# First modulation made as columns, x normalised and turned tile by tile, parameters and narrow weights laid out as runs, first weights in four loads, running sums behind the evictions

## What is computed

```python
cond = jax.nn.silu(c)                                  # c: 1 x 1024
mod = cond @ ada_w[layer] + ada_b[layer]               # 1024 x 6144
sh1, sc1, g1, sh2, sc2, g2 = [m[:, None, :] for m in jnp.split(mod, 6, axis=-1)]
h = rms_norm(x, norm_mix[layer]) * (1 + sc1) + sh1     # x: 512 x 1024
qa, ka, va, ga, za, qkvb, ab, bb, zb = _split(h @ w_in, AB_SPLITS)
```

## Time and profile before

| | before |
|---|---|
| time, median of 3 runs | 1469.92 us (1468.84 to 1470.89) |
| the profiled execution's own time | 1473.01 us |
| its span in the trace | 1470.8 us |
| PE busy | 1282.0 us (87%) |
| DVE busy | 1099.5 us (75%) |
| ACT busy | 700.2 us (48%) |
| first product of the projections | at 42.5 us |
| end of block n = 0 | at 77.8 us |
| end of `project_ab` on PE | at 244.7 us |

### The profile page before, as it was taken

One profiled execution on the slowest core, in us unless ns is written; L12 is line 12 of the kernel. 1 busy time (PEld: TensorE's weight loads), 2 busy tenths in 40 slices (PEclk: granted clock), 3 DMA queues, 4 the chain that ended last, 5 costly groups with the idle time before them and its releaser, 6 DMA issues. The chain is left out here.

```text
span 1470.8 us, 15601 instructions
## 1 busy us (share of the span) xinstructions
PE 1282.0 (87%) x6032; PEld 974.7 (66%) x6032; DVE 1099.5 (75%) x1340; ACT 700.2 (48%) x899; POOL 301.6 (21%) x125
## 2 busy tenths in 40 slices
PE   5886997869999959999999968986898799999992
PEld 3565885659884557888888854444446588888882
DVE  2756886667783666999999946967357499999994
ACT  3221334122251316777777814127422377777770
POOL 2000000000000001466455410000000145645431
PEclk9998998879999959999999978997996799999996
DMA  9688536011603267999999646354006499999944
GB/s 336 221 292 276 190 100 198 32 44 58 258 1 129 75 231 264 374 387 383 373 378 367 232 162 234 121 208 171 0 29 257 151 366 378 377 389 383 382 189 187
DMA packets 63728, 337.65 MB, mean 230 GB/s; under 512 B 11837, under 2 KB 12350, under 8 KB 49572
## 3 DMA queue, kind: packets, MB, share of 16 engines
q1 hardware_dynamic: 51428, 311.00, 57.1%
q0 software_dynamic: 11360, 22.39, 4.3%
q10 hardware_dynamic: 864, 3.23, 0.6%
HBM read 325.11 MB, written 28.84 MB: 241 GB/s over the span
## 5 line engine op out<-in xcount | busy, mean ns | idle before, releaser
L2491 DVE TENSOR_TENSOR ring_r<-ring,early_mod_r 128x2048 fp32r<-128x2048 f32 x76 | 197.8, 2633 | 25.7 <-ACT early_mod_r L1594 25.2
L1441 PE MATMUL ps<-ring_r,work_r 128*128 128x512 f32 x536 | 212.2, 396 | 0.0
L1594 ACT ACTIVATE work<-ps 128x512 f32<-128x512 f32 (+3 forms) x125 | 84.7, 683 | 236.0 <-PE ps L1441 133.0
L1439 PE MATMUL ps<-early_mod_r,work_r 128*128 128x512 f32 x468 | 187.7, 401 | 10.3 <-DVE work_r L2794 4.7
L1440 PE MATMUL ps<-early_mod_r,work_r 128*128 128x512 f32 x468 | 183.7, 393 | 0.0
L1594 ACT ACTIVATE work_r<-ring 128x2048 fp32r<-128x2048 f32 (+2 forms) x87 | 133.8, 1558 | 95.6 <-PE ps L955 95.0
L852 POOL TENSOR_TENSOR work<-work,early_mod 128x1024 f32<-128x1024 f32 x30 | 142.7, 4756 | 146.6 <-ACT work L1594 146.6
L1594 ACT ACTIVATE early_mod_r<-ring 128x2048 fp32r<-128x2048 f32 x79 | 147.5, 1908 | 0.3 <-PE ps L1441 0.2
L1439 PE MATMUL ps<-work_r 128*128 128x512 f32 x324 | 132.2, 408 | 6.8 <-DVE work_r L2794 4.7
L946 PE MATMUL ps<-const,work 128*128 128x128 f32 (+1 forms) x680 | 100.1, 289 | 41.1 <-DMA work<-h_rows,row_i 11.7
L1440 PE MATMUL ps<-work_r 128*128 128x512 f32 x324 | 128.8, 397 | 0.0
(11 more groups left out here) (334 smaller groups left out, 2452.3 us busy)
## 6 DMA issues: line engine op xcount, KB each, us to landing
ring<-in_moe_w_up_dram SPq DMA_DIRECT2D x33, 2048.0 KB, 10.0
early_mod<-in_ada_w_dram SPq DMA_DIRECT2D x80, 512.0 KB, 4.5
ring<-in_moe_w_gate_dram SPq DMA_DIRECT2D x19, 2048.0 KB, 9.7
hT<-in_moe_w_down_dram SPq DMA_DIRECT2D x16, 2048.0 KB, 9.7
ring<-in_moe_w_down_dram SPq DMA_DIRECT2D x15, 2048.0 KB, 9.9
work<-in_moe_w_gate_dram SPq DMA_DIRECT2D x14, 2048.0 KB, 10.1
ring<-in_ab_w_in_dram SPq DMA_DIRECT2D x7, 2048.0 KB, 9.5
ring<-in_ada_w_dram SPq DMA_DIRECT2D x3, 2048.0 KB, 20.4
```

Source lines behind the costliest of these rows:

```text
L1439: mm(out, a_lo, w_hi, start=first_, stop=False)
L1441: return mm(out, a_hi, w_lo, start=False, stop=last_)
L1594: return nc.scalar.activation(out, in_, fn, **kw)
L2491: v.tensor_tensor(half_of(l, m, half, True), half_of(l, m, half), highs[(2 * m + half) % MHIGHS].bitcast(F32), ALU.subtract).then_inc(SV.s ...
```

## The change

The pieces of the modulation are made as columns directly: PE takes 128 columns of a row block of `ada_w` as weights and `cond` as a single moving column, 16 products for the four row blocks and 4 for `part[i]`, each with one output column; the bias comes as columns with `cond` and is added by DVE. The repeated `cond`, the diagonal and the reduction go. Each tile of x gets its own root, is scaled by DVE into `h` and turned by PE as a plain transpose; ACT puts tile t - 1 away after it has squared tile t. On PE all four turns now stand ahead of the modulation's products. The first weights of `project_ab` come in four loads of 512 KB with a semaphore each. The parameters are laid out on the host as one block, and it and the early constants are loaded by SP behind the four pieces of `ada_w`; the narrow weights are laid out so that each partition's are one run. In `project_ab` the sums of a quarter follow its copies, and `per_step` is changed.

```diff
-        per_step = {0: (0, 0, 3, 3), 1: (0, 0, 0, 0), 2: (3, 3, 3, 3), 3: (2, 3, 2, 3), 4: (1, 1, 1, 2), 5: (1, 1, 1, 2), 6: (1, 1, 1, 2), 7: (2, 2, 1, 0)}
+        per_step = {0: (0, 0, 2, 2), 1: (0, 0, 0, 1), 2: (3, 3, 3, 2), 3: (3, 3, 3, 2), 4: (1, 1, 1, 2), 5: (1, 1, 1, 2), 6: (1, 1, 1, 2), 7: (2, 2, 2, 0)}
...
+        def narrow(of, c):
+            return of[:, c % RING].rearrange("p k f -> p (k f)")[:, 0:KD * SMALL].rearrange("p (k f) -> p k f", k=KD)
...
-                    free(c)
-                    sp.dma_start(slot(c)[:, :, 0:RANK], rows(a["ab_w_in"][0], slice(C_GA, C_GA + RANK))
-                                 ).then_inc(small_in, 16)
-                    load(c, slot(c)[:, :, RANK:RANK + 8], rows(a["ab_w_in"][0], slice(C_AB, C_AB + 8)))
+                    load(c, narrow(ring, c).rearrange("p k f -> p (k f)"), a["small_cols"])
...
-            load_ab(0)
+            for q in range(4):
+                sp.dma_start(ring[:, 0, 2 * q:2 * q + 2], rows(a["ab_w_in"][0], slice(0, 512))[:, 2 * q:2 * q + 2]).then_inc(ab0_in[q], 16)
             load_first(2)
             load_first(3)
+            sp.dma_start(block_in, a["params"]).then_inc(early_in, 16)
+            sp.dma_start(early_mod[:, 0:NEARLY], a["consts"][:, 0:NEARLY]).then_inc(early_in, 16)
...
-            param(w2aug[0:SMALL + 1, :], a["gate_rows"])
-            param(conv_w.rearrange("p c k -> p (c k)"), a["conv_cols"])
-            param(gla_gain, bc(a["gla_norm"][0]))
...
-            param(dt_bias, bc(a["gdn_dt_bias"][0]))
             param(pos_i[:], a["pos_cols"])
...
-            def first_weights(i):
+            def first_sums(i):
+                b = bank(first_bank[i])
                 pe.wait_ge(ada_in[i], 16)
-                for k in range(4):
-                    mm(bank(first_bank[i]), cond_rep[:, k], ada[i][:, 4 + k], start=(k == 0), stop=False)
-            def first_sums(i):
-                n = FIRST[i]
-                mm(bank(first_bank[i]), cst("ones")[0:1, :], first_bias[:, 512 * n:512 * n + 512], start=False, stop=False)
+                for k in range(4, KD):
+                    for j in range(4):
+                        mm(b[:, j:j + 1], ada[i][:, k, cols(j)], cond[:, k:k + 1], start=(k == 4 and j == 0), stop=False, skip_group_check=True)
                 pe.wait_ge(FIRST_DVE.sem, FIRST_DVE.at(0, f"k3{i}"))
-                mm(bank(first_bank[i]), cst("ones"), part[i], start=False, stop=True).then_inc(FIRST_PE.sem, FIRST_PE.one(f"m{i}"))
-            def turn_scaled(t):
-                pe.wait_ge(norm_dve.sem, norm_dve.at(0, f"dg{t}"))
+                for j in range(4):
+                    ins = mm(b[:, j:j + 1], part[i][:, cols(j)], cst("ones", 0, 1), start=False, stop=(j == 3), skip_group_check=True)
+                ins.then_inc(FIRST_PE.sem, FIRST_PE.one(f"m{i}"))
+            def turn_first(t):
+                pe.wait_ge(norm_dve.sem, norm_dve.at(t, "xn"))
                 if t >= 2:
-                    pe.wait_ge(norm_act.sem, norm_act.at(0, f"ev{t - 2}"))
+                    pe.wait_ge(norm_act.sem, norm_act.at(t - 2, "ev"))
                 for k in range(KD):
-                    ins = mm(bank(4 + 2 * (t % 2) + k // 4)[:, cols(k % 4)], x[:, t, cols(k)], scaled_ident[:, t], start=True, stop=True)
-                ins.then_inc(norm_pe.sem, norm_pe.one(f"t{t}"))
+                    ins = turn(bank(4 + 2 * (t % 2) + k // 4)[:, cols(k % 4)], h[:, t, cols(k)])
+                ins.then_inc(norm_pe.sem, norm_pe.one("t"))
             def first_norm():
-                pe.wait_ge(FIRST_DVE.sem, FIRST_DVE.at(0, "rep"))
                 pe.wait_ge(const_in, 16)
-                first_weights(0)
-                turn_scaled(0)
-                turn_scaled(1)
-                pe.wait_ge(bias_in, 16)
+                for t in range(TT):
+                    turn_first(t)
+                pe.wait_ge(cond_dve.sem, cond_dve.at(0, "silu"))
                 first_sums(0)
-                turn_scaled(2)
-                turn_scaled(3)
-                first_weights(1)
                 first_sums(1)
             def first_rest():
-                pe.wait_ge(norm_act.sem, norm_act.at(0, "ev3"))
+                pe.wait_ge(norm_act.sem, norm_act.at(TT - 1, "ev"))
                 for i in (2, 3):
-                    first_weights(i)
                     first_sums(i)
...
-                if qi % 4 == 0:
+                if qi < 4:
+                    act.wait_ge(ab0_in[qi], 16)
+                elif qi % 4 == 0:
...
             def first_norm():
+                def put_turned(t):
+                    act.wait_ge(norm_pe.sem, norm_pe.at(t, "t"))
+                    b = 4 + 2 * (t % 2)
+                    f(xnT[:, :, cols(t)], ps[:, b:b + 2].rearrange("p b (k n) -> p (b k) n", k=4)).then_inc(norm_act.sem, norm_act.one("ev"))
                 table(ACT.Abs_reciprocal_sqrt)
                 for t in range(TT):
+                    c = slice(t, t + 1)
                     act.wait_ge(x_tile_in[t], 16)
                     if t:
-                        act.wait_ge(norm_act.sem, norm_act.at(0, f"ss{t - 1}"))
-                    f(junk_wide, x[:, t], ACT.Square, accum_out=ss[:, t:t + 1]).then_inc(norm_act.sem, norm_act.one(f"ss{t}"))
-                act.wait_ge(norm_dve.sem, norm_dve.at(0, "var"))
-                f(rstd[:], var[:], ACT.Abs_reciprocal_sqrt).then_inc(norm_act.sem, norm_act.one("root"))
-                for t in range(TT):
-                    act.wait_ge(norm_pe.sem, norm_pe.at(0, f"t{t}"))
-                    b = 4 + 2 * (t % 2)
-                    f(xnT[:, :, cols(t)], ps[:, b:b + 2].rearrange("p b (k n) -> p (b k) n", k=4)).then_inc(norm_act.sem, norm_act.one(f"ev{t}"))
+                        act.wait_ge(RN_ACT.sem, RN_ACT.at(t - 1, "sq"))
+                    f(junk_wide, x[:, t], ACT.Square, accum_out=ss[:, c]).then_inc(RN_ACT.sem, RN_ACT.one("sq"))
+                    act.wait_ge(RN_DVE.sem, RN_DVE.at(t, "var"))
+                    f(rstd[:, c], var[:, c], ACT.Abs_reciprocal_sqrt).then_inc(RN_ACT.sem, RN_ACT.one("rs"))
+                    if t:
+                        put_turned(t - 1)
+                put_turned(TT - 1)
...
-            nc.scalar.dma_start(early_mod[:, 0:NEARLY], a["consts"][:, 0:NEARLY]).then_inc(early_in, 16)
...
-            def put_first(i):
-                S = FIRST_COL
-                dve.wait_ge(FIRST_PE.sem, FIRST_PE.at(0, f"m{i}"))
-                if i:
-                    dve.wait_ge(S.sem, S.at(0, f"cl{i - 1}"))
-                v.tensor_tensor(spread, bank(first_bank[i], 4, P), ident.unsqueeze(1).to_broadcast([P, 4, P]), ALU.mult).then_inc(S.sem, S.one(f"dg{i}"))
-                dve.wait_ge(S.sem, S.at(0, f"dg{i}"))
-                v.tensor_reduce(first_cols[:, i], spread, AX.X, ALU.add).then_inc(S.sem, S.one(f"cl{i}"))
...
-            def first_scales(half):
+            def first_scale(half):
                 S, i, c = FIRST_COL, 2 * half, slice(4 * half, 4 * half + 4)
-                put_first(i)
-                put_first(i + 1)
-                dve.wait_ge(S.sem, S.at(0, f"cl{i + 1}"))
-                v.scalar_tensor_tensor(out=scale_col[:, c], in0=first_cols[:, i], scalar=1.0, in1=gain_col0[:, c], op0=ALU.add, op1=ALU.mult)
-                v.tensor_copy(shift_col[:, c], first_cols[:, i + 1]).then_inc(S.sem, S.one(("lo", "hi")[half]))
-                dve.wait_ge(S.sem, S.at(0, ("lo", "hi")[half]))
+                dve.wait_ge(FIRST_PE.sem, FIRST_PE.at(0, f"m{i}"))
+                v.tensor_tensor(scale_sum[:, half], bank(first_bank[i])[:, 0:4], bias_col[:, KD + 4 * half:KD + 4 * half + 4], ALU.add).then_inc(S.sem, S.one(f"sum{half}"))
+                dve.wait_ge(S.sem, S.at(0, f"sum{half}"))
+                v.scalar_tensor_tensor(out=scale_col[:, c], in0=scale_sum[:, half], scalar=1.0, in1=gain_col0[:, c], op0=ALU.add, op1=ALU.mult).then_inc(S.sem, S.one(f"scale{half}"))
+            def first_shift(half):
+                S, i, c = FIRST_COL, 2 * half + 1, slice(4 * half, 4 * half + 4)
+                name = ("lo", "hi")[half]
+                dve.wait_ge(FIRST_PE.sem, FIRST_PE.at(0, f"m{i}"))
+                v.tensor_tensor(shift_col[:, c], bank(first_bank[i])[:, 0:4], bias_col[:, c], ALU.add).then_inc(S.sem, S.one(name))
+                dve.wait_ge(S.sem, S.at(0, name))
...
-                v.tensor_copy(cond_rep, cond[:, 4:8].unsqueeze(2).to_broadcast([P, 4, P])).then_inc(FIRST_DVE.sem, FIRST_DVE.one("rep"))
-                variance()
-                refine_rstd()
-                dve.wait_ge(const_in, 16)
                 for t in range(TT):
-                    v.tensor_scalar(scaled_ident[:, t], ident, rstd[:, t:t + 1], None, ALU.mult).then_inc(norm_dve.sem, norm_dve.one(f"dg{t}"))
+                    row_root(0, t)
+                    v.tensor_scalar(h[:, t], x[:, t], rstd[:, t:t + 1], None, ALU.mult).then_inc(norm_dve.sem, norm_dve.one("xn"))
                 first_parts(0)
                 first_parts(1)
```

(38 more changed lines are left out.)

69 lines of the change are left out of this document (26 added, 43 removed).

## The result

The changed kernel took 1476.84 us, the median of 5 runs (1474.02 to 1478.67), and the kernel before, run beside it, 1468.84 us in 5 runs: ratio 1.0054, 95% interval 1.0035 to 1.0073. It is 8 us slower, where 6.5 us faster was forecast, and outside the range. The profiled execution of the changed kernel (1474.02, span 1472.1) is the fastest of its runs, that of before (1473.0) lies above all of its own, so the two traces differ by only 1.3 us in span; single steps are what they can be compared by.

The account below looks back on a forecast made before the run. PE was taken to bound the kernel, with waits for DVE in the first 245 us. Beginning -4.5, blocks 1 to 3 +4.2, +4.9 and +1.9 made 6.5 us faster: 1469.9 to 1463.4 us, range 1452 to 1471.

Parts of the forecast that it names:

- whatever the change gains or loses by the start of block 4 goes through to the end: Blocks 4 to 7 keep their 98 us of busy PE, so any earlier shift reaches the end whole.
- gain 4.9: Block 2: sums put behind the copies bring the copies 4.9 us sooner; PE idles 2 us instead of 7.0.
- gain 1.9: Block 3: three sums leave the head of the copies, so it takes 26.3 us for 28.2; bounds 0 and 5.
- a wait of 5 us or more ahead of block 3: Sign that the prediction is wrong; a PE wait of 2 us for the copies was expected there.
- first projection: Beginning: pieces 0 and 1 at the low clock end at 39.4, so the first projection starts at 42.5 us, as before.
- pieces 2 and 3: Inside block 0: 40 one-column products, clock falling after 3.6 us, take 13.0 us where 10.7 were needed before.
- end of block 0 against 77.8: Block 0 ends at 82.3 us, 4.5 later than before, its other quarters losing 2.2 us to a low start.
- block 1, end of block 0 to block 2: Block 1: without the wait at its head, a chain of 7.1 us remains, against 11.3 before.
- high from the turns on: Rival: turns lift the clock, the first projection starts at 33.5 and the total is 1444 us; chance 0.12.
- gain of 4.2: Block 1: copies first removes the wait at its head, so it gains 4.2 us.
- the loads pace the sums after all: Rival: sums in blocks 2 and 3 wait 4 us more each, 8 of 11.0 us go, 1471 us; chance 0.09.
- The slower rival: Clock stays low through the rest of block 0: 14.7 us more, 8.2 slower than before, 1478 us; chance 0.06.

Follow-up runs that it names:

- before_work_64: The kernel before with only the parameter area 16 floats longer (NPAR 1112 to 1128), so `work` starts 64 bytes later; ratio to before 1.0061.
- after_work_1024: The changed kernel with NPAR 1128 to 1368, so `work` starts 1024 bytes later than before ("`work` at +1024"); 1465.39 us, ratio to before 0.9997.
- sums_later: The changed kernel with `work` 1024 bytes later and 8 sums for 11 in each of blocks 2 and 3, six moved into blocks 4 to 6; 1454.32 us, 0.9907.
- clock_kept: The changed kernel, `work` 1024 bytes later, zero-products among turns and columns, 32 columns of pieces 2 and 3 within the first quarter; 1462.65 us, 0.9969.
- columns_between: The changed kernel, `work` 1024 bytes later, one-column products reordered between turns and between products of the first two quarters, nothing added; ratio to before 0.9981.
- after_work_128: The changed kernel with NPAR 1128 to 1144, so `work` starts 128 bytes later than before; ratio to before 1.0063.

## Why the prediction was wrong

Two steps failed. The first is "whatever the change gains or loses by the start of block 4 goes through to the end". In the profile after, block 4 started 4.1 us sooner and blocks 4 to 7 kept their 98 us, but the span was 1.3 us longer: I took the same instructions later on for the same time, and the length of the parameter area had moved `work` by 64 bytes, which the prediction does not name. It cost 9 us by itself (`before_work_64`). By an estimate, 4.3 ns for about 3100 products would be 13 us, so part of it fell into waits of PE; no run separates them.

The second is the term "gain 4.9" and "gain 1.9" of blocks 2 and 3. Without the shift the forecast would have failed all the same: the two blocks gave 0.4 us together for 6.8, and the time did not change (0.9997). The prediction's own sign of being wrong, a wait of 5 us or more ahead of block 3, came: 5.05 us in the profile after, 5.9 with `work` at +1024.

By the sum's own terms, measured with `work` at +1024 so that the shift is out (in brackets: the profile after), against the one profile of before that the prediction used:

| term | forecast | measured |
|---|---|---|
| first projection | 42.5 | 41.7 (38.5) |
| pieces 2 and 3 | 13.0 | 13.9 (12.8) |
| end of block 0 against 77.8 | 4.5 later | 3.3 later (1.3) |
| block 1, end of block 0 to block 2 | 7.1 | 7.3 (7.2) |
| block 2, gain | 4.9 | 1.1 (1.4) |
| block 3, gain | 1.9 | -0.7 (-0.1) |
| start of block 4 | 6.5 sooner | 1.2 sooner (4.1) |

The before column is one execution, and an early one: in the five profiles with the beginning of before, block 0 ends at 77.8 to 80.2, and in the four of them that also have its table block 4 starts at 145.8 to 147.0. So 1.2 us sooner is within what the kernel before does by itself.

- *The clock.* Right in price: a product took 0.43 us low and about 0.2 high, and the fall in pieces 2 and 3 came as forecast. In eight of nine profiles with this beginning, pieces 0 and 1 ran low throughout and the first projection started at 41.1 to 41.8. The ninth is the one shown above, with the clock up for 3.0 us of piece 0. The prediction left it to a rule whether turns alone lift the clock, and gave 0.12 to it. In three of the nine it rose with nothing but turns before it: at 20.7 us in the profile after, at 14.8 in `after_work_1024` and at 15.2 in `sums_later`. In the last two it fell again at 18.2 and 18.7, behind a wait of PE of some 2.3 us, before the columns came. A turn took 213 ns from start to start at the low level and 109 at the high one, as the third and fourth tile show in `after_work_1024`:

```profile
17.40 1.21 PE L936 MATMUL ps<-const,work 128*128 128x128 f32 x8 [2.37 <-DVE work L2125]
19.77 1.97 PE L936 MATMUL ps<-const,work 128*128 128x128 f32 x8 [1.16 <-DVE work L2125]
```

  So the rival "high from the turns on" was nearer than it looked: the level came, but didn't last into or through the columns. The Trainium skill, page "TensorE: Matmul & The Clock Gate", section "Part 4: PE-mode transpose", says that full clock does not engage in the mode of the turns. Six of the nine profiles agree with that and these three do not; the measurement decides.
- *Block 1.* Right in its length, 7.3 for 7.1. Its gain of 4.2 was counted from the early end of block 0 in that one profile; in the other four with the beginning of before, block 1 took 8.8 to 9.4 us and not 11.3, which leaves a gain of 1.5 to 2.
- *Blocks 2 and 3.* In mechanism the rival "the loads pace the sums after all" was the case; I gave it 0.09. I had the row for it (DVE waiting 3.13 and 4.01 us for data) and took the sums behind the copies to be out of the way. But the sums of the earlier quarters still stand ahead of the next subtraction, and when their data are late, the subtraction, the products and so the copies are late with them.
- *The slower rival* (clock low through block 0) did not happen; in the profile after the clock was back at 65, 5.2 us after dense products began again.

## What to carry to other kernels

A diff that changes a size moves every area behind it: compare start addresses before and after, keep operands that are multiplied together a multiple of 256 bytes apart (0, 256, 512 and 1024 were the fast distances here), and look at the step of identical products elsewhere before explaining a loss by order. Moving work behind a critical step on an in-order queue helps only if what stays ahead of it does not wait: count the loads per block, and thin them where the queue waits for data. Here that was one line, worth 9 us in the kernel before and 13 in the changed one, more than the whole change was forecast to bring.

## What the runs showed of the hardware

- The step of back-to-back fp32r products with 512 columns depends on the distance between the streamed operand and the weights: 227 ns at multiples of 256 bytes, 229 to 234 ns on average at 32, 64, 96, 128 and 192. The Trainium skill, page "TensorE: Matmul & The Clock Gate", section "Step-by-step: what each phase is for", says that loading the next weights doesn't take read bandwidth from the running product, because there are two read ports. These runs differ from that by 1 to 3% of the step, and the measurement decides; what is shared inside was not shown.
- One-column products between dense ones ran at either level: four among dense products were high, and eight behind each of four groups of six dense products kept the granted clock at 1.00 (45 to 57 us in `clock_kept`). With 12 of them behind the second such group it fell as the third group ended, at 45.2 us, and came back at 69 (`columns_between`). What decides stays open.
- Turns alone lifted the clock in some executions and not in others: in three of nine profiles with the same beginning, and in `columns_between` at 14.5 us, after 16 turns and nothing else. What decides stays open here too.
- The granted clock ahead of its first recorded change is no guide: from 24 to 26 us it reads 1.00 in `after_work_128`, where the first change stands at 47.2, and 0.50 in `after_work_1024`, with 11 records of the same one-column products in both. The spacing of like records told the level.
